# A two-layer decoder trunk on one core: the pad behind shift_out cut from 48 to 16 columns

## The reference

```python
for layer in range(DEPTH):
    if layer == N_A_LAYERS:
        kv_mod = (c_act @ kv_ada_w + kv_ada_b).reshape(B, 2, D)
        h_kv = modulate(rms_norm(x, kv_norm_g), kv_mod[:, 0], kv_mod[:, 1])
        kv_bands = shared_kv_bands(h_kv, kv_w, cos, sin)
    mod = (c_act @ ada_w[layer] + ada_b[layer]).reshape(B, N_SUBLAYERS, 3, D)
    h = modulate(rms_norm(x, norm_g[layer, 0]), mod[:, 0, 0], mod[:, 0, 1])
    x = x + 0.5 * mod[:, 0, 2][:, None, :] * swiglu(h, ffn_w_gate[layer, 0], ffn_w_up[layer, 0], ffn_w_down[layer, 0])
    ...
def swiglu(h, w_gate, w_up, w_down):
    return (jax.nn.silu(h @ w_gate) * (h @ w_up)) @ w_down
```

## Time and profile before

| | |
|---|---|
| median of 3 runs | 2478.32 us (2477.01 to 2484.09) |
| profiled execution | 2477.01 us, its span 2475.3 us |
| TensorE clock granted, mean | 0.996 |
| PE busy | 2431.6 us, 98% |
| PEld busy | 2022.0 us, 82% |
| DVE busy | 1377.7 us, 56% |
| ACT busy | 868.7 us, 35% |
| POOL busy | 141.5 us, 6% |
| DMA moved | 408.79 MB, 165 GB/s in the mean |

### The profile page before, as it was taken

The page is one execution under the profiler, slowest core; times in us unless marked ns, Lnnn a source line. Parts: engine busy times, 40 slices in busy tenths (PEclk is TensorE's granted clock), DMA queues, the critical chain, the costliest instruction groups (busy, mean ns, idle before and its releaser), DMA issues. The chain is left out here.

```text
span 2475.3 us, 33243 instructions
## 1 busy us (share of the span) xinstructions
PE 2431.6 (98%) x11997; PEld 2022.0 (82%) x11997; DVE 1377.7 (56%) x2105; ACT 868.7 (35%) x1230; POOL 141.5 (6%) x128
## 2 busy tenths in 40 slices
PE   9999999999999999999999999999999999999998
PEld 6888888888778888888888888888788887888886
DVE  7555446677675654465545555446667667433333
ACT  3222224445443332233333333223444444333221
POOL 0000000212000000011211000000211100000000
PEclk9999999999999999999999999999999999999999
DMA  6666532665446554336557656445888973222332
GB/s 253 192 188 194 166 119 93 212 191 182 138 153 196 187 179 139 103 114 214 185 190 245 192 182 198 127 122 153 246 219 223 241 216 96 92 93 95 102 93 85
DMA packets 135715, 408.79 MB, mean 165 GB/s; under 512 B 17088, under 2 KB 17472, under 8 KB 135616
## 3 DMA queue, kind: packets, MB, share of 16 engines
q1 hardware_dynamic: 122560, 357.16, 47.9%
q0 software_dynamic: 13056, 50.33, 5.7%
HBM read 353.95 MB, written 52.43 MB: 164 GB/s over the span
## 5 line engine op out<-in xcount | busy, mean ns | idle before, releaser
L337 DVE TENSOR_TENSOR w_lo<-w_raw,w_hi 128x1024 fp32r<-128x1024 f32 (+2 forms) x386 | 471.3, 1222 | 599.5 <-ACT w_hi L333 599.2
L342 PE MATMUL ps<-h_hi,w_hi 128*128 128x512 f32 x1872 | 744.8, 398 | 8.6 <-DVE w_lo L337 4.1
L344 PE MATMUL ps<-h_hi,w_lo 128*128 128x512 f32 x1872 | 732.1, 391 | 0.0
L343 PE MATMUL ps<-h_lo,w_hi 128*128 128x512 f32 x1872 | 731.4, 391 | 0.0
L333 ACT CAST w_hi<-w_raw 128x1024 fp32r<-128x1024 f32 (+2 forms) x388 | 395.4, 1019 | 749.4 <-PE ps L344 731.2
L342 PEld LDWEIGHTS ps<-h_hi,w_hi 128*128 128x128 f32 x1872 | 353.1, 189 | 84.0 <-DVE w_lo L337 7.1
L344 PEld LDWEIGHTS ps<-h_hi,w_lo 128*128 128x128 f32 x1872 | 352.4, 188 | 75.1
L343 PEld LDWEIGHTS ps<-h_lo,w_hi 128*128 128x128 f32 x1872 | 353.2, 189 | 66.8 <-issue 0.2
L342 PE MATMUL ps<-act_hi,w_hi 128*128 128x512 f32 x704 | 275.3, 391 | 0.2 <-DVE w_lo L337 0.2
L344 PE MATMUL ps<-act_hi,w_lo 128*128 128x512 f32 x704 | 274.1, 389 | 0.0
L343 PE MATMUL ps<-act_lo,w_hi 128*128 128x512 f32 x704 | 273.9, 389 | 0.0
(11 more groups left out here) (162 smaller groups left out, 2801.4 us busy)
## 6 DMA issues: line engine op xcount, KB each, us to landing
w_raw<-gate_up SPq DMA_DIRECT2D x176, 512.0 KB, 3.7
ada_raw<-ada SPq DMA_DIRECT2D x144, 512.0 KB, 4.5
w_raw<-down SPq DMA_DIRECT2D x80, 512.0 KB, 3.6
w_raw<-kv_w SPq DMA_DIRECT2D x48, 512.0 KB, 3.5
w_raw<-mixa_w SPq DMA_DIRECT2D x34, 512.0 KB, 3.9
w_raw<-mixb_w SPq DMA_DIRECT2D x34, 512.0 KB, 5.9
kb<-rot_st POOLq DMA_DIRECT2D x12, 1024.0 KB, 5.0
k_hi<-kb SPq DMA_DIRECT2D x64, 192.0 KB, 4.9
```

The source lines that it names most:

```text
L337: eng.tensor_tensor(w_lo[:, slot, 0:n], w_raw[:, slot, 0:n], w_hi[:, slot, 0:n].bitcast(F32), ALU.subtract).then_inc(w_lo_done[slot], 2)
L342: nc.tensor.matmul(out_ap, l_hi, r_hi, start=start, stop=False, skip_group_check=skip)
L343: nc.tensor.matmul(out_ap, l_hi, r_lo, start=False, stop=False, skip_group_check=skip)
L344: return nc.tensor.matmul(out_ap, l_lo, r_hi, start=False, stop=stop, skip_group_check=skip)
```

## The change

The allocation of shift_out becomes 16 columns wide. The slice of it that is used stays the first two columns.

```diff
         eps = sb(ctx, "eps", [P, 1])
         shift_hl = sb(ctx, "shift_hl", [P, KT, 2], F32R)
-        shift_out = sb(ctx, "shift_out", [P, 48])[:, 0:2]
+        shift_out = sb(ctx, "shift_out", [P, 16])[:, 0:2]
         idle = sb(ctx, "idle", [P, S], BF16)
```

## The result

The changed kernel takes 2497.1 us in the median of 5 runs (2494.9 to 2501.13), the kernel before 2478.32 us (2476.94 to 2484.09). The ratio is 1.0072, with a 95% interval of 1.0054 to 1.0088. The change costs 18.8 us, and I had forecast none. The time lies 3.1 us above my range. Of the forecasts on record rival A's, 2504 us, is the nearest.

A forecast was written before the change was run, and what follows sets the result against it. PE was taken as the bound: number of matmuls times the distance between starts, 227 ns in the down projection. Terms 0 (PE), 0 (DVE, ACT) and -0.3 us (DMA) gave a predicted median of 2478.0 us, range 2468 to 2494.

The forecast's parts named there:

- rival A: 3216 down-projection and kv matmuls: reads at unequal starts hinder each other, 8 ns each, 2504 us; chance 0.17.
- first term: PE's 3216 down-projection and kv matmuls on moved tiles: taken as 0, ends 26 us more and 35 us less.
- Rival B: Moved fp32 matmuls lose the 11 ns over bf16, blamed on the 128-byte offset: 2443 us, or half, 2460; chance 0.07.
- Rival C: DMA and the mixers give back PE's and ACT's waits: 8 us faster, 2470 us; chance 0.04.
- The second term: DVE and ACT work on moved tiles: taken as 0, 4 us either way; ada_acc stays at 1280 ns.
- The third term: DMA loads and stores of moved tiles: slightly shorter waits, -0.3 us, ends -2 and +2.

The follow-up runs named there:

- e_112: Kernel before with shift_out 112 columns wide instead of 48, everything behind it 256 bytes later: 2480.43 us, ratio 1.0.
- the scan: Kernel before plus 14 end blocks of 32 fp32 matmuls at varied starts, other engines quiet: streamed +32 columns 8.31 us, +64 8.17 us.
- e_all128: Kernel before with a pad ahead of x, every tile 128 bytes later, so all large tiles start at multiples of 256: 2480.39 us, ratio 1.0004.
- block 3: Block of 32 matmuls in the last scan, (weights, streamed operand) alternating between (0, 0) and (32, 32) columns: 8.43 us.
- last scan: Kernel before plus 21 end blocks of 32 fp32 matmuls of 512 columns, offsets of weights and streamed operand varied: 8.16 us with all offsets 0.
- block 4: Block of 32 matmuls in the last scan, (weights, streamed operand) alternating between (0, 32) and (32, 0) columns: 8.23 us.
- second scan: Kernel before plus end blocks of 24 matmuls at finer streamed offsets, other widths and bf16: 6.37 us for fp32, 512 columns, at +0.

## Why the prediction was wrong

**The step that failed** is in the first term, PE, where I wrote that the rows nearest to the case are those of act_hi and h_hi themselves, "so I take 0". They are no rows of the case: all their pairs have the same start modulo 256 bytes, and they could only show that distances which are multiples of 256 cost nothing. That was right (e_112, 1.0). Of the offset itself they said nothing. I had said so in the same paragraph and then let them decide. The term measures 5.3 ns on 3216 matmuls, 17 us: the stream meets the load of weights that start 128 bytes off. It lies between the bounds of -11 and +8 ns, but by luck, since neither row has anything to do with unequal starts.

**Rival A** was the right mechanism in the right place, with 0.17 of chance. It said that the stream and the weights' load get in each other's way at unequal starts, and that it would show from 2.3 ns a matmul on. Its price of 8 ns was 50% too high. It came from a stretch in which all starts are equal, so something else slows that stretch, and that it came as near as it did is luck. Its second half, ACT's or DVE's reads of w_raw, has no part: the scan shows the loss without them. What I held against it, record lengths that are alike at different distances, was no evidence, for the reason above. **Rival B** is refuted: with everything at a multiple of 256 the fp32 records stay at 391 ns (e_all128), so the 11 ns between fp32 and bf16 don't come from the offset. The gap that the Trainium skill gives for 512 columns ("TensorE: Matmul & The Clock Gate", "Back-to-back issue gap") is met here by bf16 (216 ns) and by fp32 at none of the offsets tried (227 ns at the best). The section calls that gap the one of an isolated matmul, and puts a stream of weight loads and matmuls at about 131 ns. No run here shows such a pace: the keep-busy matmuls at 216 ns have a weight load each (151 PEld records for 151 matmuls in the kernel before). **Rival C** didn't happen; PE's idle time rose by 1.3 us.

**The second term** was right: ada_acc has 1279 ns, DVE as a whole 1376.2 us against 1377.7.

**The third term** had the sign right and no weight. The first queue went from 47.9% of 2475.3 us to 47.1% of 2493.9, 0.9% less time; the second, POOL's stores out of moved tiles, from 141 to 130 us, 8% less. PE got none of it, since its waits for DMA hardly changed (k_lo 4.4 us for 4.5). The first queue's 0.9% isn't the alignment's doing: with all tiles at multiples of 256 (e_all128) that queue takes 47.7% of 2483.2 us, as long as before. The rule of the Trainium skill ("DMA: Bandwidth & Descriptors", "How a descriptor splits into AXI transactions") agrees in direction for the stores, which read at the moved address, and its 3% is below the 8% seen.

**The range** ended at 2494 by a value that I chose, 5 ns, inside a bound of 8 that I had written down. The whole bound would have held the time.

## What to carry to other kernels

A change of a tile's size moves every tile behind it, and on a PE that is never idle a few nanoseconds a matmul are the whole result: look at the distance of the starts, and compare the address of the streamed operand with that of the weights that are loaded beside it. Here fp32 matmuls of 512 columns want both at the same offset modulo 256 bytes; bf16 doesn't care, and with 256 or 128 columns nothing was lost. And rows that all share one value of a quantity can't price a change of it: keep the whole bound in the range, and give the rival that the rows can't speak to its share.

## What the runs showed of the hardware

- A stream of fp32 matmuls of 512 columns takes 227 ns each when the streamed operand and the weights start at the same offset modulo 256 bytes, and 232 to 233 when they differ by 128 bytes; most of it hangs on the weights that are loaded while the stream runs (8.4 ns for block 3 of the last scan, 2.2 for block 4).
- With 512 columns of fp32, of the 19 starts of the second scan (every 16 bytes up to +240, and +4, +8 and +72 bytes) +0 was the fastest with 6.37 us a block and +64 bytes the next with 6.39; +4 bytes was the slowest with 6.55, 7.5 ns a matmul.
- At 256 columns the order turns: from start to start a block takes 3.62 us at +192 bytes against 3.74 at equal starts. At 128 columns and in bf16 nothing moves, but 128 columns take 3.51 us a block, only 0.23 us less than 256, so there the length of the stream hardly sets the pace.
- The stores on POOL's queue take 5.2% of the DMA engines' time in the changed kernel and with all tiles moved together, where they read at multiples of 256 bytes, and 5.7% before and with 112 columns (about 130 us against 141).
- Open: why the two reads hinder each other at all, which no run shows; why 64 bytes cost as much as 128 where kv_h is streamed (396 and 395 ns) and 2.2 ns in the down projections; why the loss on h is 4.5 ns and not 5.3; and what the 2.2 ns of block 4 are.
